# Turning x and the mLSTM heads in 32 by 32 squares on VectorE instead of whole on TensorE

## What is computed

```python
h = rms_norm(x, norm_g) * (1.0 + scale) + shift        # the norm runs over a token's 1024 features
proj = h @ w_in                                         # 4096 x 1024 times 1024 x 4104
pool_out = causal_pool_mixer(u) * silu(z_pool)          # windows of 2, 4, 8, 16 tokens, per-group map
q, k = silu(causal_depthwise_conv(proj[q and k columns]))
hm = mlstm_chunkwise(q, k, v, ig, lf)                   # 4 heads of 128, chunks of 128 tokens, carried memory
hm = hm * rsqrt(mean(hm * hm, axis=-1) + EPS)           # per token and head
mlstm_out = hm * mh_norm_g * o_gate * silu(z_mlstm)
x = x + gate * (concat[pool_out, mlstm_out] @ w_out)
return rms_norm(x, final_g)
```

## Time and profile before

| | |
|---|---|
| median of 3 runs | 1849.21 us (1849.15 to 1852.01) |
| the profiled execution | 1848.88 us, span 1847.1 us |
| PE busy | 1809.6 us, 98% of the span |
| VectorE busy | 1013.3 us, 55% |
| ScalarE busy | 521.5 us, 28% |
| GpSimd busy | 262.1 us, 14% |
| the DMA queue of SP | 129028 packets, 312.56 MB, 50.9% of 16 engines |

### The profile page before, as it was taken

One profiled execution on the slowest core, in us unless ns is written; L12 is line 12 of the kernel. 1 busy time (PEld: TensorE's weight loads), 2 busy tenths in 40 slices (PEclk: granted clock), 3 DMA queues, 4 the chain that ended last, 5 costly groups with the idle time before them and its releaser, 6 DMA issues.

```text
span 1847.1 us, 25117 instructions
## 1 busy us (share of the span) xinstructions
PE 1809.6 (98%) x9537; PEld 1554.0 (84%) x9537; DVE 1013.3 (55%) x2247; ACT 521.5 (28%) x1054; POOL 262.1 (14%) x229
## 2 busy tenths in 40 slices
PE   6989999999999999999999999999999999999998
PEld 5878889888898888988888888888889888898886
DVE  6685684527736276353863357452673627735383
ACT  3344331332323132222222223132222313222221
POOL 3433222040210003000030001200022000300000
PEclk9899999999999999999999999999999999999999
DMA  9896735595256552665427653466535665266431
GB/s 329 272 313 181 239 116 181 165 327 194 93 189 194 191 186 85 211 203 178 155 91 242 203 193 104 163 204 216 179 99 189 187 198 189 78 212 202 150 124 69
DMA packets 144348, 336.85 MB, mean 182 GB/s; under 512 B 13068, under 2 KB 55012, under 8 KB 144228
## 3 DMA queue, kind: packets, MB, share of 16 engines
q1 hardware_dynamic: 129028, 312.56, 50.9%
q10 hardware_dynamic: 15200, 22.68, 4.1%
HBM read 288.86 MB, written 46.33 MB: 181 GB/s over the span
## 4 chain that ended last, share of the span: by engine, by line
PE 88%; DVE 7%; issue 2%; ACT 1%; DMA 1%; SPq 0%; POOL 0%; ACTq 0%; DVEq 0%; POOLq 0%
PE ps_acc L511 23%; PE ps_acc L513 23%; PE ps_acc L512 23%; PE ps_kv L511 2%; PE ps_kv L512 2%; PE ps_kv L513 2%; PE ps_num L728 1%; PE ps_kv L732 1%; PE ps_num L727 1%; PE ps_sco L708 1%; PE ps_num L524 1%; PE ps_num L511 1%; PE ps_num L513 1%; PE ps_num L512 1%; PE ps_bro L740 1%
## 5 line engine op out<-in xcount | busy, mean ns | idle before, releaser
L511 PE MATMUL ps_acc<-sb_hT_hi,sb_w_split 128*128 128x512 f32 x1536 | 608.9, 396 | 0.7 <-POOL sb_w_split L1104 0.7
L513 PE MATMUL ps_acc<-sb_hT_hi,sb_w_split 128*128 128x512 f32 x1536 | 599.6, 390 | 0.0
L512 PE MATMUL ps_acc<-sb_hT_lo,sb_w_split 128*128 128x512 f32 x1536 | 598.5, 390 | 0.0
L513 PEld LDWEIGHTS ps_acc<-sb_hT_hi,sb_w_split 128*128 128x128 f32 x1536 | 288.5, 188 | 62.1
L511 PEld LDWEIGHTS ps_acc<-sb_hT_hi,sb_w_split 128*128 128x128 f32 x1536 | 289.0, 188 | 58.5 <-POOL sb_w_split L1104 0.8
L512 PEld LDWEIGHTS ps_acc<-sb_hT_lo,sb_w_split 128*128 128x128 f32 x1536 | 289.1, 188 | 56.9
L1116 POOL TENSOR_TENSOR sb_h_rs<-sb_h_var,sb_mhalf 128x4 f32<-128x4 f32 x32 | 32.4, 1013 | 1019.1 <-DVE sb_h_var L1546 1019.1
L1104 POOL TENSOR_TENSOR sb_w_split<-sb_w_raw,sb_w_split 128x512 fp32r<-128x512 f32 (+1 forms) x64 | 89.0, 1400 | 183.4 <-ACT sb_w_split L812 183.3
L1454 DVE SCALAR_TENSOR_TENSOR sb_acc_cv<-sb_shifted,sb_par,sb_acc_cv 128x512 f32<-128x512 f32 x96 | 76.9, 801 | 60.8 <-ACT sb_acc_cv L964 58.3
L1480 DVE TENSOR_TENSOR sb_oz<-sb_tanh,sb_oz 128x512 f32<-128x512 f32 x32 | 22.2, 692 | 150.5 <-ACT sb_tanh L980 150.5
L511 PE MATMUL ps_acc<-sb_wo_hi,sb_mixm_hi 128*128 128x512 f32 x256 | 103.3, 404 | 0.0
(11 more groups left out here) (219 smaller groups left out, 2867.9 us busy)
## 6 DMA issues: line engine op xcount, KB each, us to landing
sb_w_split<-w_kept SPq DMA_DIRECT2D x328, 512.0 KB, 4.0
sb_w_split<-w_kept SPq DMA_DIRECT2D x56, 520.0 KB, 4.8
w_kept<-sb_w_split SPq DMA_DIRECT2D x40, 512.0 KB, 6.1
sb_x_res<-x SPq DMA_DIRECT2D x34, 512.0 KB, 5.5
sb_w_raw<-w_in SPq DMA_DIRECT2D x64, 256.0 KB, 5.1
out<-sb_qT SPq DMA_DIRECT2D x32, 512.0 KB, 2.9
sb_x_in<-x SPq DMA_DIRECT2D x30, 512.0 KB, 5.8
sb_ada_raw<-w_ada SPq DMA_DIRECT2D x8, 1024.0 KB, 9.6
```

The source lines that it names most:

```text
L511: pe.matmul(dst, st_hi, mv_hi, start=start, stop=False)
L512: pe.matmul(dst, st_hi, mv_lo, start=False, stop=False)
L513: return pe.matmul(dst, st_lo, mv_hi, start=False, stop=stop)
```

## The change

For blocks 1 to 7, x is loaded in squares: partition 32q + r of the tile gets, for the eight feature groups k and the four token groups j, the 32 features 128k + 32q to 128k + 32q + 31 of token 32j + r. That takes four transfers of 1024 runs of 128 bytes for each chunk, where there was one transfer of 128 runs of 4 KB. One VectorE transpose of 32 by 32 squares over [128, 1024] (`prep_turn`) then gives feature rows. A token's features now lie on four partitions, so ScalarE sums four pieces per partition, and one matmul with a 0/1 matrix (`same_row`) adds the four partitions (`x_sums`); its result lies in the PSUM bank that the heads no longer use, and for a block's last chunk in a corner of `ps_kv`. The scaling moves to ScalarE. The heads are turned in squares by VectorE (`head_turn`), written to DRAM, and read back in four transfers of 512 runs of 128 bytes, which put the squares in their places (`keep_hm`, `load_hm`, on ScalarE's queue). Turned x and turned heads lie in `kT` (whose layout becomes [128, chunk, head, 128]) and in `dmat` and `q_in`, which now are one tile. The first block's x is turned as before.

```diff
@@ SP @@
-                sp.dma_start(dst[:, c % 2, :], x[0, bass.ds(nb * BLK + c * P, P), :]).then_inc(x_loaded[c % 2], 16)
+                if c >= 2 or nb > 1:
+                    sp.wait_ge(x_turned, (nb - 1) * NC + c - 1)
+                else:
+                    sp.wait_ge(x_T, PREPS)
+                tokens = x[0, bass.ds(nb * BLK + c * P, P), :].rearrange("(j r) (k q n) -> r k j q n", r=32, q=4, n=32)
+                for q in range(4):
+                    dst = x_in[32 * q:32 * q + 32, c % 2, :].rearrange("r (k j n) -> r k j n", k=KT, j=NC)
+                    sp.dma_start(dst, tokens[:, :, :, q, :]).then_inc(x_loaded[c % 2], 16)
...
                     load_x(b + 1, 2)
+                    load_x(b + 1, 3)
+                    load_w(b, UNITS)
                 store(b, 0)
-                if not last:
-                    load_w(b, UNITS)
-                    load_x(b + 1, 3)
@@ PE @@
+            def x_sums(nb, c):
...
+                pe.wait_ge(x_sq_done, nb * NC + (c + 1))
+                pe.matmul(x_sums_at[c], same_row[:, :], x_sq[:, NC * (c % 2):NC * (c % 2) + NC], start=True,
+                          stop=True).then_inc(x_summed, 1)
...
-                    if j > 0:
-                        hm_transposed(j - 1)
                     numerator_and_update(j)
+                    if j >= 2 and not last_block:
+                        x_sums(b + 1, j - 2)
...
                 out_m(1)
-                prep_next(0)
-                prep_next(1)
                 for i in range(8):
                     if i > 1:
                         out_m(i)
                     out_p(i)
-                    if i == 1:
-                        hm_transposed(3)
-                    if i in (2, 4, 6):
-                        prep_next(i)
-                        prep_next(i + 1)
+                    if i in (1, 3) and not last_block:
+                        x_sums(b + 1, i // 2 + 2)
@@ ScalarE @@
+                def keep_hm(j):
+                    act.wait_ge(hm_turned, b * NC + (j + 1))
+                    act.dma_start(hm_kept[j % 2].rearrange("p (h n) -> p h n", h=NH), kT[:, j, :, :]).then_inc(hm_kept_done, 16)
+
+                def load_hm(j):
+                    act.wait_ge(hm_kept_done, 16 * (b * NC + (j + 1)))
+                    squares = hm_kept[j % 2].rearrange("(t c) (h d r) -> c h t d r", c=32, h=NH, r=32)
+                    for d in range(4):
+                        dst = kT[32 * d:32 * d + 32, j, :, :].rearrange("c h (t r) -> c h t r", r=32)
+                        act.dma_start(dst, squares[:, :, :, d, :]).then_inc(hm_loaded, 16)
...
+                    if j > 0:
+                        keep_hm(j - 1)
                     src, free = acc_wait("zp", j)
...
                     act.activation(tanh[:, :], src[:, :], ACT.Tanh, scale=0.5).then_inc(tanh_ready, 1)
+                    if j > 0:
+                        load_hm(j - 1)
+                    if j == 3 and not last_block:
+                        prep_scale(b + 1, 0)
@@ VectorE @@
+            def prep_turn(nb, c):
...
+                dve.wait_ge(x_scaled, nb * NC + (c + 1))
+                reach(dve, h_lo, nb * PREPS + 2 * (c - 2) + 2)
+                V.transpose(x_turned_to[c % 2].rearrange("p a b t -> p (a b) t") if c % 2 else x_turned_to[0],
+                            x_in[:, c % 2, :]).then_inc(x_turned, 1)
...
+                def head_turn(j):
+                    in_turn()
+                    V.transpose(kT[:, j, :, :], hm[:, :, :]).then_inc(hm_turned, 1)
```

More of the change, by code:

```diff
@@ L309, in chunk, with x_count, four_k, hT_part @@
             return slice(P * j, P * j + P)
+        def x_count(nb, c):
+            return 32 + 128 * (nb - 1) + 64 * (c // 2 + 1) if nb else 16 * (c // 2 + 1)
+        def four_k(c, half):
+            return x_turned_to[c % 2][:, 2 * half:2 * half + 2, :, :]
+        def hT_part(t, c, half):
+            return t[:, 4 * half:4 * half + 4, chunk(c)].rearrange("p (a b) t -> p a b t", b=2)
+        def by_chunk(t):
+            return t.rearrange("p (c t) -> p c t", t=P)
         def col(t, n, m=P):
@@ L513, in split3 @@
                 return pe.matmul(dst, st_lo, mv_hi, start=False, stop=stop)
[L515 to L525, removed]
+            def x_sums(nb, c):
+                if nb == 1 and c == 0:
+                    pe.wait_ge(same_row_ready, 1)
+                pe.wait_ge(x_sq_done, nb * NC + (c + 1))
+                pe.matmul(x_sums_at[c], same_row[:, :], x_sq[:, NC * (c % 2):NC * (c % 2) + NC], start=True,
+                          stop=True).then_inc(x_summed, 1)
             pe.wait_ge(cst_loaded, 16)
@@ L707, in heads_to_scores @@
                     for h in range(NH):
-                        last = pe.matmul(sco[:, chunk(h)], kT[:, h, chunk(j)], qT[:, h, chunk(j)], start=True, stop=True)
+                        last = pe.matmul(sco[:, chunk(h)], kT[:, j, h, :], qT[:, h, chunk(j)], start=True, stop=True)
                     last.then_inc(sco_full, 1)
@@ L715, in keys_transposed @@
                     for h in range(NH):
-                        last = pe.transpose(kv[1][:, chunk(h)], kT[:, h, chunk(j)], ident)
+                        last = pe.transpose(kv[1][:, chunk(h)], kT[:, j, h, :], ident)
                     last.then_inc(k_T, 1)
@@ L734, in numerator_and_update @@
                     last.then_inc(kv_done, 1)
[L736 to L741, removed]
                 for j in range(NC):
@@ L840, in _ @@
                     reach(act, x_sq_done, c)
-                    prep_sq(0, c, (x_in, x_res)[half])
+                    square_first(c)
                 for c in (2 * half, 2 * half + 1):
@@ L1152, in one_block @@
                         h_rsqrt(j - 1)
+                    if j == 3 and not last_block:
+                        x_rsqrt(b + 1, 0)
                     for n in range(m, m + 4):
@@ L1167, in one_block @@
                         rsqrt(o_var_done, b * NC + (j + 1), o_rs[:, j % 2:j % 2 + 1], o_var[:, j % 2:j % 2 + 1], o_rs_done)
+                    if i == 5 and not last_block:
+                        prep_lo(b + 1, 6)
+                        prep_lo(b + 1, 7)
             one_block(0, False, True)
@@ L1217, in prep_full @@
+            def prep_full(nb, p):
+                in_turn()
+                dve.wait_ge(x_turned, (nb - 1) * NC + (p // 2 + 1))
                 for i in range(4):
-                    k = 4 * (p % 2) + i
-                    last = V.tensor_scalar(full[p % 2][:, i, :], num[p % 2][:, chunk(i)], gain[:, k:k + 1], shift[:, k:k + 1],
-                                           ALU.mult, ALU.add)
+                    k, at = 4 * (p % 2) + i, four_k(p // 2, p % 2)[:, i // 2, i % 2, :]
+                    last = V.tensor_scalar(at, at, gain[:, k:k + 1], shift[:, k:k + 1], ALU.mult, ALU.add)
@@ L1343, in _ @@
             step(V.memset(den[:, :], 0.0))
+            step(V.tensor_reduce(same_row[:, 0:32], ident.rearrange("p (q c) -> p c q", q=4), AX.X, ALU.add))
+            in_turn()
+            V.tensor_copy(same_row[:, 32:P].rearrange("p (q c) -> p q c", q=3),
+                          same_row[:, 0:32].unsqueeze(1).broadcast_to([P, 3, 32])).then_inc(same_row_ready, 1)
+            did(same_row_ready, 1)
             setup_steps = count[0]
@@ L1628, in one_block @@
                         head_norm(j - 1)
+                    if j == 3 and not last_block:
+                        prep_var(b + 1, 0)
                     in_turn()
@@ L1645, in one_block @@
                         m_low(0)
-                    if j >= 2 and not last_block:
-                        prep_var(b + 1, j - 2)
                     in_turn()
@@ L1687, in one_block @@
                     step(V.memset(warm[:, :, :], 1.0))
+                if not last_block:
+                    prep_var(b + 1, 1)
+                    prep_turn(b + 1, 0)
                 heads(3)
```

190 lines of the change are left out of this document (113 added, 77 removed).

## The result

| | before | after |
|---|---|---|
| median | 1849.18 us (4 runs) | **1888.92 us** (4 runs, 1887.44 to 1893.8) |
| profiled execution's span | 1847.1 us | 1886.7 us |
| a middle block | 219.74 us | 223.30 us |

A middle block is the mean of six: the time from the issue of block 0's third store to that of block 6's, over six.

A forecast was written before the change was run, and what follows sets the result against it. The prediction took PE, busy 98% of the span, to bound the kernel: 1848.9 - 39.6 (transposes removed) + 4.6 (`x_sums`) + 23.8 (PE waiting for VectorE's residual) = 1837.7, 1838 us, range 1815 to 1862.

The forecast's parts named there:

- the heads of chunk 0: Chunk loop of block 4: their trip through DRAM lands by 1107.85, so VectorE's mix ends at 1108.6, 0.65 us late.
- chunk 1's heads to be in time: Chunk loop of block 4: VectorE mixes chunk 1's heads without waiting and starts chunk 3 work at 1125.55, 0.37 us late.
- where PE wants the residual's bank: At `out_m(2)`, PE waits for VectorE's first residual addition: 3.4 us in each of seven blocks, 23.8 us.
- late heads: Rival, chance 0.08: the heads' DRAM exchanges come 2 us later at two mixes, 4 us on VectorE's path, 1866 us.
- 5.41 - 0.66 - 3.4: Per block on PE: 5.41 us of transposes removed, 0.66 us of `x_sums` added, 3.4 us of waiting added.
- VectorE's path: Block 4, from the first mix of heads through the turns to the first residual's end, put at 1148.9.
- The turns: VectorE's transposes of squares: 1.24 us for 1024 columns of x, 0.69 us for 512 of heads, taken from plain passes.
- dear squares: Rival, chance 0.07: VectorE's turns take 1.25 us more for x and 0.55 for heads; PE's wait is 7.5, time 1866.
- Dear short transfers: Rival, chance 0.18: at 29 ns per 128-byte run, PE waits 6.0 us in `x_sums` for x's squares, 42 in all, 1856.
- the prediction's line: DMA time per run against its size, through 117 ns at 2422 bytes and 29 at 455; 15 ns at 128 bytes.
- Their issues: Loads of x at the chunk loop's start: eight issues on SP, 3.6 us instead of 0.91, costed at nothing.
- multiply and add after the turn ... no gain: VectorE's step after x's turn, after the first residual: reads SBUF instead of PSUM, counted as no gain.

The follow-up runs named there:

- experiment 7: The changed kernel with each x chunk loaded by one transfer in whole rows of 4 KB instead of four in runs of 128 bytes; 1891.38 us.
- experiment 8: The kernel of experiment 4 with the first mixed heads' high and low parts, `y_low(3)` and the first residual addition moved, none removed; 1865.76 us.
- experiment 4: The changed kernel with each mix of the heads some 12 us later, all instructions and transfers kept; 1858.25 us.
- experiment 9: The kernel of experiment 8 with the sum of x's third chunk and all that follows from it one output tile later; 1860.35 us.

## Why the prediction was wrong

**The step that failed** is the one on the heads of chunk 0: "ScalarE's tanh ends at 1102.9; by then the DRAM write (2.5 us) is over. Four issues at 0.45 each ... A quarter of 256 KB should land no later than the shortest 256 KB read, 3.6 us". In the time base of before (21.17 us earlier than after: the end of the zp tile in chunk 1) ScalarE could issue the reads only at 1105.1, since the write took 5.7 us. The 2.5 was the median of writes in another stage; the largest of the same row, 5.4, was the one that fitted, since chunk 0's write took 4.8 to 6.7 us in the eight blocks, with the DMA engines at a share of 0.96 or more while it ran. At the end of the loop and in the output stage of this block, at a share of 0.35, the same write lands in 2.0 us, as this group of the changed kernel shows (DMA issues of 1156 to 1176 us, last number median us to landing):

```profile
hm_kept<-sb_kT ACTq DMA_DIRECT2D x2, 256.0 KB, 2.0
```

The four issues took 2.67 us instead of 1.8, and the last landing 2.46 instead of 3.6 (4.3 to 6.2 in blocks 0, 5, 6 and 7). So the mix of chunk 0 ended at 1110.4 instead of 1108.6, and then, where the forecast took chunk 1's heads to be in time, a second wait of 2.23 us came: the chunk 3 work started at 1129.6 instead of 1125.55, 4.1 us late against the forecast.

**What that cost.** The forecast charged lateness only where PE wants the residual's bank, and had PE never wait in the loop. In block 4 PE waits 0.67 us in chunk 3 for VectorE's memory step and 2.42 us at that chunk's numerator (1156.47), runs at the lower clock for part of the next 4.3 us (0.66), and then still waits 1.23 us for `y_low(3)` and 0.34 for the residual. The rival "late heads" had the mechanism, "a write, a wait on ScalarE and four reads, in competition with weights", and its 4 us are close to the 5.1 measured in the mean middle block. That is in part luck, since it had 2 us at two mixes and most blocks have one wait, of 1.9 or of over 5 us. It had 0.08 of the chances and 1866 us. Of the 23 us that it is short of the result, 21 can be named: 7 are the middle blocks' 5.1 in place of 4, 6 are block 0, 3 the last block, which it left out, and 5 the loss in block 0 that is there without the trip (below). In block 0 ScalarE and GpSimd split the weights besides; the four issues took 4.1 us and the last landing 6.2, PE waited 8.09 us, and its clock was at 0.67 for the next 8 us; the trip has cost 9.8 us by that block's third store. The bounds of rows 7, 2.0 and 5.4, should have gone into the sum's range: with 5.4 from the write's issue (1099.4 in that time base), 1.35 to the last of the four issues and 3.6, the landing is at 1109.8 and VectorE waits 2.6 us at the first mix instead of 0.65. That is 13 us in seven blocks, where the forecast had gained 11.

**What held.** The rest of the sum comes out, as the kernel without the trip shows. In a middle block the forecast was 5.41 - 0.66 - 3.4 = 1.35 us gained, and it gained 219.74 - 218.17 = 1.57; the total, 1843, is 5 us over the forecast, and these too were lost at block 0 (310.45 against 306.07 for the third store). VectorE's path held as well: in block 4 its first residual ends at 1150.40, which is 1148.5 in the time base of before (1.89 us earlier, by the scores of chunk 0), and the forecast had 1148.9. But PE does not stand in one place for 3.4 us there. It waits 1.50 us ahead of `out_p(0)` for `y_low(3)`, which the forecast had not put on PE's path although it stands ahead of that residual on VectorE, and 0.43 us for the residual. Of the 3.2 us that the mean block lost (5.41 - 0.66 - 1.57), these are 1.9; the rest shows in no wait of PE. Over the program of that kernel:

```profile
PE ps_acc L542 <- DVE sb_mixp_lo L1639: 10.6, 7, 1.7
PE ps_acc L542 <- DVE sb_x_res L1739: 2.9, 6, 0.6
```

So the path through VectorE was the right one, and the place of PE's wait was not. The turns are as estimated, 1.25 us for 1024 columns and 0.71 for 512:

```profile
L1633 DVE STREAM_TRANSPOSE sb_kT<-sb_hm 128x512 f32<-128x512 f32 x32 | 22.8, 711 | 1.1
L1277 DVE STREAM_TRANSPOSE sb_kT<-sb_x_in 128x1024 f32<-128x1024 f32 x14 | 17.4, 1245 | 2.2 <-ACT sb_x_in L842 1.7
```

So "dear squares" fell, and the figure of the Trainium skill for one 128x128 bf16 turn (VectorE: DVE Perf Modes, The three transpose paths), scaled up to 2.5 us, is twice too large for this operation here. "Dear short transfers" fell too. The queue of SP took 53.2% x 16 x 1886.7 - 50.9% x 16 x 1847.1 = 1017 us of its 16 engines more. With the 688 us of the 28 x 128 runs of 4 KB that went (192 ns each by the prediction's line) that is 1705 us for 28 x 4096 runs, 15 ns each, the value taken and not the 29 of the rival; experiment 7 shows that they cost no time. Their issues were taken too cheap: the eight at the start of block 4's loop kept SyncE's queue for 8.0 us, where the sum had 3.6. PE still waited for no weight in that loop. Yet what that rival said PE would do, wait in `x_sums` for ScalarE's squares, came true once the rest was out of the way (experiment 8). Whether the short runs had a part in that wait no run tests; that ScalarE waited 18 us less for these squares in experiment 7, 2.6 in each of seven blocks, speaks for it.

**A point that was too kind**: "multiply and add after the turn ... no gain". It was a small loss. From PSUM the eight of a chunk took 2.77 us in every place (404 ns each by the profile of before, overlapped); from SBUF in place they take 3.24 us in three of a block's four chunks and 2.27 in the other, 0.9 us more in a block:

```profile
1174.39 3.24 DVE L1287 TENSOR_SCALAR sb_kT<-sb_kT,sb_gain,sb_shift 128x128 f32<-128x128 f32 x8
...
1183.63 2.27 DVE L1287 TENSOR_SCALAR sb_dmat_q_in<-sb_dmat_q_in,sb_gain,sb_shift 128x128 f32<-128x128 f32 x8
1185.94 2.31 DVE L1760 SCALAR_TENSOR_TENSOR sb_qT<-sb_x_res,sb_o_rs,sb_fg 128x1024 f32<-128x1024 f32 x1
```

## What to carry to other kernels

An exchange through DRAM is a chain of completions: write, issues, reads. Price it from transfers that ran in the same stage, beside the same weights, put the larger landing of the row into the sum, and compare its length with the time until the reader wants the data; here the first trip of each block took 9 to 15 us, had about 8 us of room, and made its reader wait for the excess. Look at several blocks before taking one as typical: block 4 waited twice, most waited once. Give such a chain room by order before work is added to it, but look at what stands next in line: here each wait that was cleared uncovered another on the same engine. And of a change with two parts, try each alone: x's part was worth 12 us, the heads' part cost 55.

## What the runs showed of the hardware

- A wait of 3.4 us on TensorE was followed by some 4.8 us at 1.2 GHz (granted clock 0.50) and cost 2.1 us more than itself (experiment 8). After 2.42 us of waiting the changed kernel had 0.66 between 1156.4 and 1160.7, after 2.10 us experiment 4 had 0.67 between 1144 and 1149; after 1.75 us experiment 9 had 1.00 throughout.
- VectorE's multiply and add from SBUF took 3.24 us while GpSimd made low halves (1176.25 to 1177.55), and 2.27 us where GpSimd was idle. GpSimd's next pair ran beside VectorE's final scaling, which took 2.31 us. In experiment 8 that scaling started first, at 1175.90, and took 1.29; it was GpSimd's piece, begun at 1176.61, that took 1.73 instead of 1.29. The Trainium skill (Trainium Architecture — The Big Picture, What this means for kernel authors) says that on the engines' side of SBUF only VectorE and GpSimd contend, through a shared port that one of them locks; the rows agree.
- The same 256 KB write of the changed kernel landed in 2.0 to 2.5 us where the DMA share while it ran was up to 0.54 (once, in block 0, in 3.6), in 3.4 to 4.7 us at 0.75 to 0.80, and in 4.8 to 6.7 us at 0.96 or more. The Trainium skill (SBUF — State Buffer, The DMA setup-cost knee) gives every transfer a fixed 2 us or so, mostly until its completion is confirmed, and by its fit 256 KB take 2.6 us, an estimate. The 2.0 measured, with the bytes in it, are less, and what the loop adds has to be read from the trace.
- Issuing one read of 512 runs of 128 bytes kept ScalarE's queue for 0.66 us (median of 128), one transfer of 128 whole rows for 0.33.
